# 512 picked tokens instead of 384 in a PEER decoder layer, with cross attention and expert selection in one stage

## The reference

```python
x = x + merged_mixers(rms_norm(x))                     # convolution and attention, unchanged
h, m = rms_norm(x), rms_norm(mem)                      # mem: 256 tokens
q, k, v = h @ w_xq, *split(m @ w_xkv)                  # 4 heads of 256
x = x + softmax(q @ k.T / 16) @ v @ w_xo
h = rms_norm(x)
q = (h @ w_pq)                                         # 8 heads, 2 halves of 128
sc = q @ sub_keys                                      # (token, head, half, 128 keys)
top_v, top_i = top_k(sc, 16)
best_v, best_i = top_k(all sums top_v[0] + top_v[1], 16)
expert = top_i[0] * 128 + top_i[1]                     # at best_i; 128 a token
gate = softmax(best_v)
x = x + sum over the 128 experts of gelu(u[expert] . h) * gate * v[expert]
out = rms_norm(x)
```

## Time and profile before

| | us |
|---|---|
| median of 3 runs (3989.51 to 4028.2) | 4000.87 |
| the profiled execution | 3974.28 |
| its span | 3972.5 |
| mixers and merge, to | 1351 |
| cross attention, to | 1652 |
| selection, to | 2690 |
| gates beside 28 expert tiles, to | 2944 |
| values and the last norm, to | 3972.5 |

### The profile page before, as it was taken

How to read it: one execution, slowest core, us unless ns; L and a number is a source line. 1 busy time by engine, 2 the same in 40 slices (tenths; PEclk the granted TensorE clock), 3 DMA queues, 4 the chain that set the end, 5 groups by cost and what they waited for, 6 DMA issues and landing times. The chain is left out here.

```text
span 3972.5 us, 61578 instructions
## 1 busy us (share of the span) xinstructions
PE 3687.8 (93%) x21687; PEld 3261.5 (82%) x21687; DVE 3061.8 (77%) x5229; ACT 1455.4 (37%) x2548; POOL 1648.2 (41%) x1269
## 2 busy tenths in 40 slices
PE   6999999999899999988998989998996999999996
PEld 5766676676577886778888989998996999999996
DVE  5676776777753503459999998978976999999998
ACT  3456555565652424222222222224541222222222
POOL 2433444333312120105655455552224556566552
PEclk9999999999899999999999999999998999999998
DMA  2111111111253311138888887895779999999995
GB/s 86 49 48 54 44 47 44 48 54 54 96 191 128 132 53 76 59 123 300 325 327 316 293 325 281 327 357 215 265 266 318 369 382 390 379 374 375 386 392 196
DMA packets 315022, 848.43 MB, mean 214 GB/s; under 512 B 27184, under 2 KB 122672, under 8 KB 310832
## 3 DMA queue, kind: packets, MB, share of 16 engines
q1 hardware_dynamic: 201328, 400.91, 29.4%
q0 software_dynamic: 110592, 402.70, 26.7%
q10 hardware_dynamic: 2880, 41.94, 2.7%
HBM read 726.96 MB, written 118.49 MB: 213 GB/s over the span
## 5 line engine op out<-in xcount | busy, mean ns | idle before, releaser
L1920 POOL DMA_INDIRECT join_urow<-in_u_rows,select_row_now x384 | 510.6, 1330 | 508.3 <-DVE join_rows L2221 223.0
L2672 POOL DMA_INDIRECT spread_vrow<-in_v_rows,spread_row_of x384 | 540.1, 1407 | 409.4 <-DVE spread_y L2740 301.8
L163 PE MATMUL spread_banks<-spread_ahi,spread_vhi 128*128 128x384 f32 (+1 forms) x2048 | 640.7, 313 | 55.7 <-DVE spread_acc L2730 40.3
L163 PE MATMUL select_products<-h_hi,shared_pair_hi 128*128 128x256 f32 (+2 forms) x1856 | 608.4, 328 | 71.5 <-DVE shared_raw_low L1736 66.3
L164 PE MATMUL spread_banks<-spread_alo,spread_vhi 128*128 128x384 f32 (+1 forms) x2048 | 638.2, 312 | 0.0
L165 PE MATMUL spread_banks<-spread_ahi,spread_vlo 128*128 128x384 f32 (+1 forms) x2048 | 638.0, 312 | 0.0
L164 PE MATMUL select_products<-h_lo,shared_pair_hi 128*128 128x256 f32 (+2 forms) x1856 | 603.2, 325 | 0.0
L165 PE MATMUL select_products<-h_hi,shared_raw_low 128*128 128x256 f32 (+2 forms) x1856 | 602.4, 325 | 0.0
L163 PE MATMUL shared_carry<-shared_wide_hi,shared_w_hi 128*128 128x512 f32 x1408 | 558.0, 396 | 27.7 <-DVE shared_wide_lo L591 11.2
L164 PE MATMUL shared_carry<-shared_wide_lo,shared_w_hi 128*128 128x512 f32 x1408 | 553.4, 393 | 0.0
L165 PE MATMUL shared_carry<-shared_wide_hi,shared_w_lo 128*128 128x512 f32 x1408 | 553.0, 393 | 0.0
(11 more groups left out here) (307 smaller groups left out, 6664.0 us busy)
## 6 DMA issues: line engine op xcount, KB each, us to landing
spread_vraw<-in_peer_v SPq DMA_DIRECT2D x124, 512.0 KB, 8.7
shared_raw<-in_select_pairs SPq DMA_DIRECT2D x112, 512.0 KB, 6.5
gates<-spread_stage ACTq DMA_DIRECT2D x20, 2048.0 KB, 7.3
spread_act<-gelu_u SPq DMA_DIRECT2D x128, 320.0 KB, 7.5
spread_graw<-gates SPq DMA_DIRECT2D x32, 1280.0 KB, 11.8
gelu_u<-front SPq DMA_DIRECT2D x100, 320.0 KB, 6.9
shared_w_raw<-in_w_mix SPq DMA_DIRECT2D x56, 512.0 KB, 3.6
shared_w_raw<-in_w_cross SPq DMA_DIRECT2D x32, 512.0 KB, 3.5
```

The lines of the kernel that those rows point to most:

```text
L163: nc.tensor.matmul(out, whi, xhi, start=(first and i == 0), stop=False)
L1920: nc.gpsimd.indirect_dma_start(picks.slots[s][:], None, u_rows, bass.IndirectOffsetOnAxis(row_now[:, t, j:j + 1], 0)).then_inc(row_loaded[ ...
L2672: nc.gpsimd.indirect_dma_start(v_slots[s][:], None, v_rows, bass.IndirectOffsetOnAxis(row_of[:, par, t, j:j + 1], 0)).then_inc(row_loaded[ ...
```

## The change

`GT` is 4 and the dense tokens are the last 512 (`TD`). The two stages of cross attention and selection become `retrieve_phase`. It has one stream of 16 + 16 + 16 + 32 + 128 weight tiles (`tile_order`): those for the questions, the output and the queries are loaded and split once for each half of the tokens, the first half being the picked one. The four carried PSUM banks go round over all products (`bank_order`). The questions of the dense half run beside the attention of the picked half; the attention of the dense half follows alone; its output product (`give`, 1) stands among the first queries. Top-k goes in 16 blocks (a head and a half), the picked half first, with 512 dots in blocks 1 to 15 from 7 slots, and the expert tiles in blocks 2 to 15. DVE makes the low parts of all query and expert tiles, POOL those for questions and output. The position search subtracts and takes minima in 16-bit integers, without the multiply.

In the last stage the gates stand alone, in 32 steps, with 4 picked rows after each; 12 rows a group remain. The products stay in all 8 PSUM banks over the 32 groups and are added once at the end. Every loop is written out, and the gates' load comes behind the fourth gelu tile. The norm is one.

```diff
-GT = 3
-HALF = (384, 256)
+GT = 4
+TD = ND * P
...
+def tile_order():
...
+    tiles = [("memory", 0, n) for n in range(KV)]
+    for half in range(2):
+        tiles += [("ask", half, k) for k in range(NC)]
+    tiles += [("give", 0, k) for k in range(NC)]
+    tiles += query(0) + query(1) + [("give", 1, k) for k in range(NC)] + query(2)
+    for b in range(FIRST_DENSE, BLOCKS):
+        for i, e in enumerate(experts_of(b)):
+            tiles.append(("expert", 1, e))
+            if i == QUERY_BEHIND and b + 1 < BLOCKS:
+                tiles += query(b + 1)
...
+            for u in range(UNITS + 1):
+                if u < UNITS:
+                    scores_of(0, u)
+                if u in (3, 5, 7):
+                    weigh(0, (u - 3) // 2)
+                if u < UNITS:
+                    tiles.product(pe, ("ask", 1, u), hhi[1], hlo[1])
+                if u:
+                    turn(0, u - 1)
...
+            for c in range(2):
+                query(0, c)
+            query(1, 0)
+            scores(0)
+            query(1, 1)
+            for k in range(NC):
+                give(1, k)
...
+            def beside(b, at):
+                upto = STARTS[b] + 2 + (STARTS[b + 1] - STARTS[b]) * (at + 1) // PLACES
+                for n in range(low_at[0], upto):
+                    if not tiles.maker[n]:
+                        tiles.split_low(dve, nc.vector, n)
...
+                tt(hit[:].rearrange("p t a (b x) -> p t a b x", x=2),
+                   placed[:].rearrange("p c t (b x) -> p (c t) b x", x=2).unsqueeze(2).to_broadcast([P, NU, K, K // 2, 2]),
+                   partf[:].unsqueeze(3).to_broadcast([P, NU, K, K // 2, 2]), ALU.subtract).then_inc(hit_step, 1)
...
-                nc.vector.tensor_tensor(acc[:, k, token_half[h]], before[:, token_half[h]], product_of(k, h), ALU.add
-                                        ).then_inc(added, 1)
...
+            for g in range(2, NG):
+                load_tile(g, 0)
+                load_tile(g, 1)
+                load_values(g, 0)
+                load_tile(g, 2)
+                load_values(g, 1)
+                load_tile(g, 3)
+                load_gates(g)
...
+                tt(low_part, low_part, twice(3, n), ALU.mult).then_inc(gated, 1)
...
+                weigh_picks(EARLY * n, EARLY * n + EARLY)
...
+                for w in range(PLACES):
+                    weigh_picks(*picks_of(g, w, PLACES))
+                    if g + 1 < NG:
+                        e, turn = divmod(w, 3)
+                        if turn == 0 and e < E:
+                            weigh(g + 1, e)
+                        if turn == 2 and e < E:
+                            split(g + 1, e)
+                    if w == 1 and g:
+                        low(g, NQ - 1)
+                    if g + 1 < NG and w in LOWS:
                         low(g + 1, LOWS.index(w))
...
+            LOWS = (4, 8, 12)
...
+                        mm = three_pass(nc, banks[:, k], [(vhi[:, q, e, dp], vlo[:, q, e, dp], ahi[g % 2][:, e], alo[g % 2][:, e])],
+                                        first=(g == 0 and e == 0), last=(g == NG - 1 and e == E - 1))
```

More of the change, by code:

```diff
@@ L1296, in cross_attention_phase @@
[L1296 to L1306, removed]
@@ L1317, in cross_attention_phase @@
-        block = m.block()
[L1319 to L1337, removed]
+        turned_done, pT_made, o_high = m.sem("turned_done"), m.sem("pT_made"), m.sem("o_high")
@@ L1360, in _ @@
[L1360 to L1366, removed]
+            sync.dma_start(x_in[:, NC - 1], xT[:, NC - 1]).then_inc(last_stored, 16)
+            sync.dma_start(gain[:], ffn_gain).then_inc(gain_loaded, 16)
@@ new lines, in _, with query, scores @@
+            weigh(1, XH - 1)
+            def query(b, c):
+                half = b // PH
+                tiles.product(pe, ("query", b, c), hhi[half], hlo[half], H, (h2_low, lambda k: k + 1) if b == 0 and c == 0 else None)
+            def scores(b):
+                if b == 0:
+                    pe.wait_ge(keys_loaded, 16)
+                    pe.wait_ge(h_copied, GT)
+                else:
+                    pe.wait_ge(sc_made, 2 * b)
+                for c in range(2):
+                    tile = ("query", b, c)
+                    pe.wait_ge(banks.emptied(tile), banks.turn(tile))
+                    for t in range(ND):
+                        mm = nc.tensor.matmul(scps[:, c, t], asked[b % 2][c][:, t * P:t * P + P], keys[:, c], start=True, stop=True)
+                    mm.then_inc(scored, 1)
@@ new lines, in _, with expert @@
+            for c in range(2):
+                query(2, c)
+            norms[1].root(nc, act)
+            for k in range(NC):
+                high(1, k)
+            copy_scores(2)
+            def expert(e):
+                tile = ("expert", 1, e)
+                act.wait_ge(banks.filled(tile), banks.turn(tile))
+                if e >= GELU_SLOTS:
+                    act.wait_ge(gelu_stored[e % GELU_SLOTS], 16 * (e // GELU_SLOTS))
+                nc.scalar.activation(bent_out[e % GELU_SLOTS], banks.at(tile), ACT.Gelu_apprx_tanh).then_inc(banks.emptied(tile), 1)
+                ahead(tile)
@@ L2321, in tail_low @@
[L2321 to L2334 removed]
+                dve.wait_ge(part_made, b * 5 + 4)
@@ L2335, in _ @@
+            dve.wait_ge(made, 3)
+            for b in range(BLOCKS):
+                body(b)
+            gates(BLOCKS - 1)
+            dve.wait_ge(part_high, 3)
+            nc.vector.scalar_tensor_tensor(out=parts[:, 3], in0=side[:, 2].unsqueeze(2).to_broadcast([P, H, 2]), scalar=GATE_SCALE, in1=parts[:, 2],
+                                           op0=ALU.mult, op1=ALU.subtract).then_inc(part_low, 1)
             dve.wait_ge(bent, 1)
-            dve.wait_ge(gate_made, PH + 1)
+            dve.wait_ge(gate_made, BLOCKS + 1)
@@ L2843, in _ @@
         @block.tensor
         def _(pe):
-            def step(n):
+            for n in range(N):
                 b = n % 3
```

2188 lines of the change are left out of this document (923 added, 1265 removed).

## The result

The changed kernel takes 4347.42 us (median of 4 runs, 4340.2 to 4348.85) against 3995.19 for the kernel before (4 runs, 3971.96 to 4028.2). The ratio is 1.0871, with a 95% interval from 1.0792 to 1.0951. It is slower, as forecast, but by 8.7% and not by 4.5%: the time lies above the upper end of the range, 4320. The profiled execution has a span of 4344.6 us, 372.1 more than before.

A forecast was written before the change was run, and what follows sets the result against it. DVE was taken to bound top-k and gates, waits for the gates' load the value groups. First maximum at 1645, blocks to 2817, gates from 2836, values to 4143 and a 28 us end gave span 4171, forecast 4180, range 3980 to 4320.

The forecast's parts named there:

- DVE in the blocks; waits: Top-k stage: DVE's top-k, dots, low parts and dense half's adds, squares and norm take 1107 us, its waits 65 (bounds 20 and 130).
- a group: Value stage: 23.6 us of DVE work plus a 6 us wait for the gates' load make 30 us.
- the 30 us of the other bound: Top-k search: extra cost if 16-bit integer steps went at one element per clock step; forecast not to come.
- The landing I take as 10 us: Value stage: the gates' load of 1 MB lands 10 us after issue, so DVE waits 6 us a group.
- my bound of 34 us (a landing of 14): Value stage: upper bound for a group, if the gates' load took 14 us to land.
- The data are never late: Rival: gates' load and picked rows land before DVE asks; groups take 23.6 us, block waits 20, total 3930; chance 0.15.
- PE becomes the bound of the blocks: Rival: in the top-k blocks PE's waits lower its clock, a block takes 78 instead of 71 us, total 4280; chance 0.13.
- Half of it: Rival: the gates come 3 us late in the value groups and blocks wait 40 us, about 4040; chance 0.10.

## Why the prediction was right in kind and wrong in size

| step | forecast | after |
|---|---|---|
| first maximum | 1645 | 1660.3 |
| DVE in the blocks; waits | 1107; 65 | 1104.0 busy of 1145; 41 idle |
| first step of the gates | 2836 | 2815.7 |
| gates | 320 | 320.2 (to 3135.8) |
| first weighing | 3178 | 3155.9, after a wait of 20.1 |
| a group | 30 | 36.6, behind the first distance |
| last rows done | 4143 | 4312.4 |
| end behind them | 28 | 32.2 |
| span | 4171 | 4344.6 |

*Up to the values every term stands within 24 us.* Of the 15 us lost before the first maximum 6 were lost ahead of the first question, whose product starts at 1412.5 and not at 1406; the rest I did not trace. They came back in the blocks, where DVE idled for 41 us and not 65, and the gates began 20 us ahead of the forecast. The search's integer steps took 1.226 us (L2163) and 0.684 (L2170), the price of the fp16 rows; the 30 us of the other bound did not come, and the Trainium skill's rule for 16-bit types ("VectorE: DVE Perf Modes", section "Mode 2×_1P") agrees with these integer rows too. The gates and the wait for the stored ones (20.1, where 22 was carried over) are as priced, so the first weighing is 22 us earlier than forecast.

*The step that failed is "The landing I take as 10 us".* It is 15.5. DVE waits 11.0 us a group and not 6. A second, smaller one was not in the sum: DVE waits 1.65 us a group for ACT's high part of `v` (26.4 us in 16 times). With 23.6 us of work that makes 36.2; 36.6 is measured. Over the 30 distances behind the first, 30 x 6.6 = 198 us are added, and 22 were given back at the first weighing: 4171 + 198 - 22 = 4347, close to the span of 4344.6. The mechanism (the load behind the fourth tile, DVE out of work, a wait in every group) was right. The size was not, and my bound of 34 us (a landing of 14) was too low, so the range ended below the result.

*Why the size failed.* I took the landing as a property of the load, scaled by its bytes. The runs show that it depends on what runs beside it: 7.4 us with no rows, 11.2 with five held back, 15.5 as written, 17.5 when issued earlier, 19.5 on a third queue, 21.6 a group ahead; and for the larger load of the kernel before 11.8 in its own place, 18.2 in that of the change. And the earlier trace rows held the warning: the longest landing, 27.8. In the kernel before that is the load whose issue stands here with POOL's first fetch and DVE's wait:

```profile
2982.25 0.97 SPq L2578 DMA_DIRECT2D spread_graw<-gates  x1
```

```profile
2978.47 0.96 POOL L2672 DMA_INDIRECT spread_vrow<-in_v_rows,spread_row_of  x1 [13.02 <-issue]
```

```profile
3010.12 0.82 DVE L2720 TENSOR_TENSOR spread_act<-spread_act,spread_graw 128x640 f32<-128x640 f32 x1 [26.79 <-DMA spread_graw<-gates]
```

It went out among the first 12 row fetches. Who asks what made the maximum of a row learns the price under load. I read the median alone. The place of the load I had priced only by DVE's work behind it, not by what it would meet there.

*The rivals.* "The data are never late" is refuted: the data decide. Its price of 23.6 us a group is not reached even with two buffers: DVE's own chain gives 25.5 there, and the bytes 26.9. "PE becomes the bound of the blocks" did not come: the granted clock was 0.94, and PE waited 124.6 us for DVE's low parts. "Half of it" neither.

*What remains of the loss* was forecast: with two buffers the first step of the gates starts 115 us later (2814.3 against 2699.0), the gates and the wait behind them take 340 us instead of 268, and the values give back 102 (865 us from the first weighing to the last row, where it was 967).

## What to carry to other kernels

A transfer that many others run beside has no landing time of its own: bound it by the longest landing in the trace and by what was issued with it, and ask which fetches the freed slots will start. When no engine of a stage is full, look for a load that may start only after the last use of its single buffer; here a second buffer, or holding other fetches back until it has landed, was worth more than an earlier place in the queue (ratios 1.023 and 1.059 against 1.088). And before work is moved from DVE to POOL, look in the trace whether DVE's steps grow while POOL works.

## What I had not expected of the hardware

A queue of its own made the gates' load no faster: 19.5 us, against 17.5 on SP's queue when it is issued at the same point of the group. An fp32 subtraction on POOL stopped a dot on DVE for its whole 2.38 us. And the granted clock in the stage of the gates was 0.57, with PE busy for 110.3 of 319 us; the stage still took the 320 us that DVE's steps alone had priced.
